# Values of the dilated attention from seven products, with turns, waits, banks and first loads moved, in a four-stage network on one Trainium2 core

## The chip, the cores and the metric

The kernel runs on one core of one Trainium2 chip. The time is that of one execution on the device, in microseconds (us), from the first instruction to the last. It is given as the median of several runs. Everything is computed in float32. The engines of a core are named as the profile names them: PE is TensorE (matrix products and transposes), with PEld for its weight loads; DVE is VectorE; ACT is ScalarE; POOL is GpSimd; SP is SyncE, which here only issues DMA transfers. A "bank" is one of the eight banks of PSUM, into which PE writes 128 x 512 values; "arena" is one big SBUF tensor that holds everything else, so that rows of the trace call nearly every operand by that name.

## The reference, cut to what matters

256 tokens of width 1024 go through two layers of a block whose mixer adds an mLSTM branch and a dilated attention, each followed by a SwiGLU, then through a windowed attention with 256 context tokens and a gated linear attention (GLA), each with an MLP of 4096. Every stage is modulated by rows computed from a condition vector `c`.

```python
c_act = jax.nn.silu(c)
h = layer_norm(x)
for l in range(DEPTH):                                  # DEPTH = 2
    ada = (c_act @ w_ada[l] + b_ada[l])[:, None, :]     # 6 x 1024 values
    sh1, sc1, g1, sh2, sc2, g2 = jnp.split(ada, 6, axis=-1)
    u = h * (1.0 + sc1) + sh1
    y = mixer(u, ...)
    h = layer_norm(DN_ALPHA * h + g1 * y, ...)
    u = h * (1.0 + sc2) + sh2
    h = layer_norm(DN_ALPHA * h + g2 * swiglu(u, w1[l], w3[l], w2[l]), ...)

# mixer: z = u @ w_in; y_a = mlstm_branch(...) @ w_a; y_b = dilated_attention(qkv_a) @ w_b
#        (sigmoid(g_a) * y_a + sigmoid(g_b) * y_b) @ w_out
def dilated_attention(qkv, slopes):       # three patterns: strides 1, 4, 16; 8 heads of 64 each
    qkv = qkv.reshape(B, S, 3, N_PATTERNS, ATT_SLOTS, ATT_HEAD_DIM)
    ...                                   # banded softmax of each pattern, then a softmax over patterns
```

The *values* of the dilated attention are `u @ w_in` for 3 x 512 columns, one group of 512 for each pattern: 256 tokens x 1024 times 1024 x 1536.

## The kernel before

**Work by stage.** One program is written out by hand for each engine, without loops on the device. Each engine runs its list in order, and semaphores tie the lists. The names in the waits are those of steps: `VA 0 full` is PE's last matmul of the tile VA 0, `VA 0 drained` the copy of its bank. PE's list sets the order. A layer goes: first values of the mLSTM ("VM", `values_of`) while the first panels of weights arrive by columns k of the contraction; the gate tile "G"; queries and keys with a convolution by DVE ("S 0" is the first score tile behind it); twelve tiles of queries and keys of the dilated attention ("AQK n"), beside which run pieces of the mLSTM (`minis`, called after each n); then the **value stage**, below; gates and outputs; SwiGLU with `up` panels; the down projection.

**Weights.** They come by SP's DMA as half panels of 4 x 512 columns (1 MB) into a ring of 7. PE frees a panel when it has run its last matmul on it.

**Seven products.** The gates, the up panels and most MLPs are computed with Strassen's scheme: the 2 x 2 blocks of the product come from 7 products of sums instead of 8 products. The order of the products is `ORDER = (1, 2, 4, 5, 7, 6, 3)`. For each panel there are four sums of weight blocks, 128x1024 each: sums 5 and 7 are made by POOL (`gate_weight_sums`, L3474 and its like), 6 and 3 by DVE (`panel_sums`); and DVE makes four sums of token blocks once (`token_sums`) and adds up the results from the banks (`first_sum`, 1 operation, and `product_sums`, 6). Products 6 and 3 overwrite weight blocks that products 1 and 2 have read.

**Value stage before.** `va(j, w)` computes one of six tiles: 128 tokens x 512 columns with 8 matmuls over 512 columns, straight from the weights, and ACT copies each bank. Between them stand the scores (`scores(u)`, u is a pair of slots, tt one of two token halves), the transposed probabilities (`turned(u)`) and the products with the values (`values(u)`). DVE runs a loop over four pairs of slots: maxima, probabilities (`probs n`), and, from the third pair on, a gate panel.

**Turns.** A turn is a piece of `c_act @ w_ada`, done by DVE: two operations of 128x1028 from a slot of weights (four where two condition vectors are needed). POOL issues the load of each slot when DVE has freed it (`ada_free`). POOL's weight sums stand in the same list, at the load numbers given in GATE_JOBS and FIRST_UP_JOB. Where DVE's turns stand is given by MINI_TURNS (after AQK tile n), by `beside_mix(1)` at the end of each pair of slots, by tuples in WA and WB, and by UP_TURNS (after up panel `at`, layer 1 only).

**Start.** `silu(c)` is a Sigmoid by ACT and a product by DVE. The first eight turns are made panel by panel (`ft` 0 to 7), each followed by a modulated column of tokens. After ft 1 DVE raises `first_free`; with that POOL issues the other condition vectors and the first two loads for turns.

**Seams.** Where a stage begins, its tokens are normalised, transposed into a bank by PE, and scaled and shifted out of it column by column, four columns by ACT and four by DVE. `drained(...)` waits for all four.

The lines of the trace: L601 is every matmul, L599 every transpose, L2268 DVE's tensor_tensor (sums), L2271 its tensor_scalar, L2274 its scalar_tensor_tensor (turns among them), L1543 and L1546 ACT's functions and plain bank copies, L3474/L3476 POOL's sums for the up panels, L3490/L3492 those for the gates, L3538 POOL's loads for turns. In the trace a matmul in float32 is two instructions.

```python
ADA_EARLY = (4, 8)                       # turns ahead of the gate tile, by layer
UP_TURNS = (3, 6)
MINI_TURNS = (2, 4, 6, 8, 9, 11)
```

## Time and profile before

| | before |
|---|---|
| median of 3 runs | 2246.53 us (2246.24 to 2246.94) |
| profiled execution, time | 2250.32 us |
| profiled execution, span | 2248.5 us |
| PE busy | 2213.8 us, 98% |
| DVE busy | 1427.2 us, 63% |
| ACT busy | 502.4 us, 22% |
| POOL busy | 287.0 us, 13% |
| clock granted to TensorE, mean | 0.998 |

The profile follows one execution. Its span leaves out what lies before the first and behind the last instruction. "Busy" of PE is an upper bound of useful work: the ends of matmuls are modelled. In a timeline a row is a stretch of like instructions of an engine: its start, its length, line, operation, form and count; the square brackets give the engine's idle time just before it, and what ended it. PEclk is the clock granted to TensorE as a part of full speed.

### The profile page before, as it was taken

The numbers are of one execution on the slowest core, as the hardware profiler recorded it, in microseconds if no ns is written. First come the engines' busy times: TensorE is split into PE (matmuls) and PEld (weight loads), VectorE is DVE, ScalarE is ACT, GpSimd is POOL, SyncE is SP. The second block draws the span as 40 slices with busy tenths as digits, with TensorE's granted clock in tenths as the row PEclk, the third lists the DMA queues.
The fourth block names the chain that finished last, engine by engine and source line by source line (L and its number), as shares of the span: only waits on it lengthen the run. The fifth ranks groups of instructions, "written<-read, shape, count | busy, mean of one in ns | idle before, by whom it ended". The sixth has DMA issues, their size and how long they took to land. (4 is left out here: it accounts for less than half of the span.)

```text
span 2248.5 us, 29974 instructions
## 1 busy us (share of the span) xinstructions
PE 2213.8 (98%) x11968; PEld 1805.9 (80%) x11968; DVE 1427.2 (63%) x2593; ACT 502.4 (22%) x1104; POOL 287.0 (13%) x181
## 2 busy tenths in 40 slices
PE   7999999999999999999999999999999999999998
PEld 5788599799868885888998655588888887778987
DVE  5685453645656566756656877775575777556655
ACT  1213230100012222201110376321200023343300
POOL 0000121331000001223220000000000002002442
PEclk9999999999999999999999999999999999999999
DMA  9995546444576655465655511433443533235542
GB/s 392 324 301 190 189 162 220 169 163 157 196 282 200 237 188 206 160 232 185 193 194 170 188 38 38 160 113 131 139 143 132 210 139 131 75 131 188 187 161 84
DMA packets 179769, 398.91 MB, mean 177 GB/s; under 512 B 21168, under 2 KB 25648, under 8 KB 176560
## 3 DMA queue, kind: packets, MB, share of 16 engines
q1 hardware_dynamic: 136736, 285.03, 36.3%
q0 software_dynamic: 24080, 93.69, 12.2%
q10 hardware_dynamic: 18816, 18.27, 2.5%
q8 instruction: 96, 1.57, 0.3%
q14 instruction: 41, 0.34, 0.0%
HBM read 395.87 MB, written 1.11 MB: 177 GB/s over the span
## 5 line engine op out<-in xcount | busy, mean ns | idle before, releaser
L601 PE MATMUL bank<-arena 128*128 128x256 f32 (+4 forms) x11384 | 2154.2, 358 | 13.2 <-ACT arena L1543 6.0
L601 PEld LDWEIGHTS bank<-arena 128*128 128x128 f32 (+2 forms) x11384 | 1739.9, 188 | 404.3 <-issue 211.8
L2268 DVE TENSOR_TENSOR arena<-arena 128x1024 f32<-128x1024 f32 (+8 forms) x576 | 479.2, 848 | 186.2 <-PE bank L601 148.3
L1543 ACT ACTIVATE arena<-arena 128x512 f32<-128x512 f32 (+5 forms) x443 | 222.6, 525 | 791.9 <-DVE arena L2268 405.2
L2274 DVE SCALAR_TENSOR_TENSOR arena<-arena 128x1028 f32<-128x1028 f32 (+6 forms) x367 | 315.5, 876 | 89.8 <-DMA arena<-in_w_ada 63.7
L2268 DVE TENSOR_TENSOR arena<-arena,bank 128x256 f32<-128x256 f32 (+2 forms) x383 | 172.5, 476 | 184.6 <-PE bank L601 173.6
L3538 POOL DMA_DIRECT2D arena<-in_w_ada x88 | 62.8, 714 | 1484.4 <-DVEq L2283 1441.5
L1543 ACT ACTIVATE arena<-bank 128x256 f32<-128x256 f32 (+3 forms) x165 | 67.3, 423 | 553.8 <-PE bank L601 552.1
L1546 ACT ACTIVATE arena<-bank 128x512 f32<-128x512 f32 (+1 forms) x165 | 89.2, 597 | 307.0 <-PE bank L601 270.7
L2268 DVE TENSOR_TENSOR arena<-bank,arena 128x512 f32<-128x512 f32 (+1 forms) x86 | 56.3, 666 | 157.8 <-PE bank L601 143.1
L2274 DVE SCALAR_TENSOR_TENSOR arena<-bank,arena 128x254 f32<-128x254 f32 (+2 forms) x184 | 78.1, 469 | 54.5 <-ACT arena L1543 27.4
L2271 DVE TENSOR_SCALAR arena<-arena 128x512 f32<-128x512 f32 (+6 forms) x258 | 81.2, 344 | 24.8 <-ACT arena L1543 18.2
L599 PEld LDWEIGHTS bank<-arena 128*128 128x128 f32 x584 | 68.0, 143 | 28.1 <-issue 24.2
L599 PE MATMUL bank<-arena 128*128 128x128 f32 x584 | 74.3, 275 | 11.6 <-DVE arena L2271 11.4
L2274 DVE SCALAR_TENSOR_TENSOR junk<-arena 128x1028 bf16<-128x1028 f32 x64 | 79.7, 1245 | 6.0 <-DMA arena<-in_w_ada 1.7
L1543 ACT ACTIVATE arena<-bank,arena 128x128 f32<-128x128 f32 (+2 forms) x138 | 57.4, 484 | 84.2 <-PE bank L599 37.5
L3474 POOL TENSOR_TENSOR arena<-arena 128x1024 f32<-128x1024 f32 x20 | 48.4, 2420 | 180.8 <-DMA arena<-in_w 86.2
L2271 DVE TENSOR_SCALAR arena<-bank,arena 128x256 f32<-128x256 f32 (+1 forms) x112 | 46.3, 468 | 26.8 <-PE bank L599 14.0
L1543 ACT ACT_TABLE_LOAD x47 | 60.3, 1283 | 2.6 <-PEq L3609 1.2
L2274 DVE SCALAR_TENSOR_TENSOR arena<-arena,bank 128x512 f32<-128x512 f32 (+1 forms) x40 | 24.5, 644 | 43.4 <-PE bank L601 42.6
L3476 POOL TENSOR_TENSOR arena<-arena 128x1024 f32<-128x1024 f32 x20 | 51.2, 2562 | 1.6
L3505 POOL TENSOR_TENSOR arena<-arena 128x1024 f32<-128x1024 f32 x14 | 35.4, 2526 | 87.0 <-PE bank L601 73.1
(39 smaller groups left out, 257.2 us busy)
## 6 DMA issues: line engine op xcount, KB each, us to landing
arena<-in_w_ada POOLq DMA_DIRECT2D x88, 1028.0 KB, 5.8
arena<-in_w_in SPq DMA_DIRECT2D x84, 1024.0 KB, 8.1
arena<-in_w SPq DMA_DIRECT2D x56, 1024.0 KB, 6.8
arena<-in_w_mlp_in SPq DMA_DIRECT2D x32, 1024.0 KB, 7.2
arena<-in_w_mlp_out SPq DMA_DIRECT2D x32, 1024.0 KB, 7.3
arena<-in_w_gla SPq DMA_DIRECT2D x12, 1024.0 KB, 7.0
arena<-in_w_ada SPq DMA_DIRECT2D x16, 514.0 KB, 19.4
arena<-in_w_a SPq DMA_DIRECT2D x8, 1024.0 KB, 7.1
```

What stands on the lines that cost most here:

```text
L599: ins = nc.tensor.transpose(out, lhsT, rhs)
L601: ins = nc.tensor.matmul(out, lhsT, rhs, start=start, stop=stop)
L1543: return nc.scalar.activation(out, x, f, **kw)
L1546: return nc.scalar.activation(out, tile(key)[:, :out.free_size()], f)
L2268: return V.tensor_tensor(out, x, y, op)
L2271: return V.tensor_scalar(out, x, s1, s2, op0, op1) if op1 is not None else V.tensor_scalar(out, x, s1, None, op0)
L2274: return V.scalar_tensor_tensor(out=out, in0=x, scalar=s, in1=y, op0=op0, op1=op1, **kw)
L3474: nc.gpsimd.tensor_tensor(up_sum(at), a21, a22, ALU.add).then_inc(up_sums_made, 1)
L3476: nc.gpsimd.tensor_tensor(a21, a11, a21, ALU.subtract).then_inc(up_sums_made, 1)
L3505: nc.gpsimd.tensor_tensor(wsum, a21, a22, ALU.add).then_inc(mlp_sums_made, 1)
L3538: pool.dma_start(adaw[:, n % ADA_SLOTS], half_source(job, q)).then_inc(ada_in[n % ADA_SLOTS], 16)
```

## The change

1. **Values.** `va` gives way to `value_products(g, order)`: the 512 columns of each pattern g are made with seven products of 4 matmuls over 256 columns. Tokens are split in halves for g = 0 and by even and odd place for g = 1 and 2. POOL makes two weight sums for each g (`value_panel_sums`), DVE two (`value_weight_sums`), four more token sums ("classes"), and seven additions from banks; ACT copies one bank for each g. The scores, transposes and value products are placed anew among them. POOL's sums for the first gates now wait for `probs 3` and `probs 5`.
2. **Turns.** More of them stand beside the AQK tiles (layer 0: nine instead of six, layer 1: seven, three of them in halves, instead of six), fewer in the loop over slots (one, at the last pair, instead of four). In layer 1 the two whole turns beside the up panels become ten halves. `token_sums("gates")` goes ahead of the last piece of mLSTM.
3. **Start.** Silu by ACT alone; `first_free` after ft 3; the banks of VM in layer 0 are those of T shifted by one.
4. **Gate tile of layer 0.** Three turns ahead of it and the fourth behind "gates abs".
5. **Seams.** Layer 1: the first three columns are waited for one by one. Seam to the GLA ("next"): the first tile of gates is computed by token half and column, the first half ahead of the second transposes; DVE's share of the first half is moved ahead of the last addition of the MLP.
6. **Windowed attention.** At t = 1 ACT drains query 3 and the turned probabilities before `latent_exps(1, 1)`.
7. **GLA.** `decays(3)` goes from the start of h = 2 to behind its state.

```diff
-UP_TURNS = (3, 6)
-MINI_TURNS = (2, 4, 6, 8, 9, 11)
+UP_TURNS = {at: (at % 2,) for at in range(10)}
+MINI_TURNS = ({n: (0, 1) for n in (0, 1, 2, 3, 4, 5, 6, 8, 9)},
+              {**{n: (0, 1) for n in range(4)}, **{n: (n % 2,) for n in range(4, 10)}})
+VALUE_JOBS = {23: [(0, g) for g in range(NPAT)], 45: [(1, g) for g in range(NPAT)]}
...
+        class_x = [UT[:, KH * j:KH * j + KH, r::RES] for j in range(2) for r in range(RES)]
...
-                        if k == 0:
+                        if k < 3:
+                            pe.wait_ge(act_done, AC.at(f"T 0 column {k}"))
+                        else:
                             drained("T 0 0")
...
+                def value_products(g, order, over=None):
+                    q = quarters(value_panel_at(l, g))
+                    x, sums, tag = value_tokens(g)
+                    ops = {1: (q[0], x[0]), 2: (q[1], x[2]), 4: (q[3], sums[4]), 5: (gate_sum, sums[5]),
+                           7: (q[2], sums[7]), 6: (q[0], sums[6]), 3: (q[1], x[3])}
+                    for i in order:
...
+                        if i in (6, 3):
+                            pe.wait_ge(dve_done, DV.at(f"VA {g} w{i}"))
+                        if i in (5, 7):
+                            pe.wait_ge(value_sums_made, values_made(l, g, i))
+                        for k in range(KH):
+                            mm(ps[:, :2 * P], ops[i][1][:, k, :], ops[i][0][:, k, :], start=(k == 0), stop=(k == KH - 1),
+                               done=key if k == KH - 1 else None)
...
                     if u == 0:
-                        for j in range(6):
-                            pe.wait_ge(act_done, AC.at(f"VA {j} drained"))
+                        for g in range(NPAT):
+                            pe.wait_ge(dve_done, DV.at(f"VA {g} c12"))
...
                 w = panel()
-                va(0, w)
+                value_products(0, ORDER[:2])
                 scores(0)
-                va(1, w)
+                value_products(0, ORDER[2:])
                 release(w)
                 w = panel()
-                va(2, w)
+                value_products(1, ORDER[:4])
                 turned(0)
+                value_products(1, (6, 7, 3), "PT 1 1")
+                release(w)
                 scores(1)
-                va(3, w)
+                w = panel()
+                value_products(2, (1, 2, 4, 5, 6, 7, 3))
                 release(w)
-                w = panel()
-                va(4, w)
-                va(5, w)
-                release(w)
+                scores(2, (0,))
+                values(0)
                 turned(1)
-                values(0)
-                scores(2)
+                scores(2, (1,))
...
-                    func(csig[0], crow[:, 0, :D], ACT.Sigmoid).then_inc(act_done, AC.step("sigmoid 0"))
+                    func(crow[:, 0, :D], crow[:, 0, :D], ACT.Silu).then_inc(act_done, AC.step("cond 0"))
...
-                        if ft == 1:
+                        if ft == 3:
                             dve.wait_ge(dve_done, DV.count)
                             dve.sem_inc(first_free, 1)
...
+                beside_gates = 3 if l == 0 else ADA_EARLY[l]
+                early_turns(turns[:beside_gates])
                 dve.wait_ge(pe_done, PE.at("G full"))
...
+                early_turns(turns[beside_gates:ADA_EARLY[l]])
                 dve.wait_ge(act_done, AC.at("softplus"))
...
+                token_sums("classes", class_x, [class_tokens[i] for i in (5, 6, 4)], False, class_tokens[7])
+                value_weight_sums(0)
+                first_sum("VA 0", value_blocks(0), value_read(0))
                 for u in range(SLOTS // 2):
...
+                    if u == 0:
+                        for _ in product_sums("VA 0", value_blocks(0), value_read(0)):
+                            pass
+                    if u == 1:
+                        value_weight_sums(2)
+                        first_sum("VA 2", value_blocks(2), value_read(2))
...
-                    beside_mix(1)
+                    if u == 3:
+                        turn_part((0, 1))
...
+            gate_columns(0, range(4))
+            normed_transposes("next", range(1, 2), None)
...
-                if h in (1, 2):
-                    decays(h + 1)
+                if h == 1:
+                    decays(2)
...
+                if h == 2:
+                    decays(3)
...
+                if p == 0:
+                    pool.wait_ge(dve_of[f"layer {l}"], DV.of(f"layer {l}", f"probs {3 + 2 * b}"))
...
-                    pool.wait_ge(pe_of[f"layer {l}"], PE.of(f"layer {l}", "S 3 full"))
+                    pool.wait_ge(pe_of[f"layer {l}"], PE.of(f"layer {l}", f"VA {NPAT - 1} 5 full"))
```

**PE, the value stage of a layer**, in program order; L599 (L621 after) are transposes (`turned`), L601 (L623) matmuls, a count is of matmuls as written in the program. The rows with 64 partitions or 128 columns are scores and value products. Before:

```order
L601 MATMUL bank<-arena 128x512 x8
L601 MATMUL bank<-arena 128x256 x2
L601 MATMUL bank<-arena 128x128 x4
...
L601 MATMUL bank<-arena 128x512 x16
L599 MATMUL bank<-arena 128x128 x16
...
L601 MATMUL bank<-arena 128x512 x24
L599 MATMUL bank<-arena 128x128 x16
```

After, the same stretch:

```order
L623 MATMUL bank<-arena 128x256 x10
L623 MATMUL bank<-arena 128x128 x4
...
L623 MATMUL bank<-arena 128x256 x36
L621 MATMUL bank<-arena 128x128 x16
L623 MATMUL bank<-arena 128x256 x14
...
L623 MATMUL bank<-arena 128x256 x30
L623 MATMUL bank<-arena 128x128 x4
```

The 48 matmuls over 512 columns are gone, and 84 over 256 stand in their place (counted in the rows with the scores' own, which have that width too); the scores of the first pair now stand behind 8 short matmuls, and the second transposes behind the first products with values.

**DVE, the value stage of layer 0**, from the token sums for the gates on. L2268 (L2320) are sums, L2274 (L2326) with 128x1028 a turn, with 512 the sum of a score bank and its bias; L2864 (L2936) a maximum, 128x512 of L2271 (L2323) probabilities. Before:

```order
L2274 SCALAR_TENSOR_TENSOR arena<-arena 128x1028 x2
L2268 TENSOR_TENSOR arena<-arena 128x512 x4
L2274 SCALAR_TENSOR_TENSOR arena<-arena,bank 128x512 x2
L2864 TENSOR_REDUCE arena<-arena 128x2
...
L2870 RECIPROCAL arena<-arena 128x2
L2271 TENSOR_SCALAR arena<-arena 128x512 x2
L2274 SCALAR_TENSOR_TENSOR arena<-arena 128x1028 x2
```

After:

```order
L2320 TENSOR_TENSOR arena<-arena 128x512 x4
L2326 SCALAR_TENSOR_TENSOR arena<-bank,arena 128x256 x2
L2320 TENSOR_TENSOR arena<-arena 128x512 x4
L2320 TENSOR_TENSOR arena<-arena 128x4x256 x2
L2320 TENSOR_TENSOR arena<-arena,bank 128x256
L2326 SCALAR_TENSOR_TENSOR arena<-arena,bank 128x512 x2
...
L2320 TENSOR_TENSOR arena<-arena,bank 128x256 x6
L2948 RECIPROCAL arena<-arena 128x2
...
L2323 TENSOR_SCALAR arena<-arena 128x512 x2
L2320 TENSOR_TENSOR arena<-arena 128x4x256 x2
L2320 TENSOR_TENSOR arena<-arena,bank 128x256 x7
```

The turns have left, and token sums, two weight sums and seven additions for each pattern have come, the first two patterns' around the first pair of slots.

**PE, the seam to the GLA.** L599 (L621) with 128x128 are the transposes of the normalised tokens, eight for each token half; the matmuls are the first tile of gates, behind them the second (16 more). Before:

```order
L599 MATMUL bank<-arena 128x128 x16
L601 MATMUL bank<-arena 128x256 x32
```

After:

```order
L621 MATMUL bank<-arena 128x128 x8
L623 MATMUL bank<-arena 128x128 x8
L621 MATMUL bank<-arena 128x128 x8
L623 MATMUL bank<-arena 128x128 x24
L623 MATMUL bank<-arena 128x256 x16
```

The first tile is now 32 matmuls over 128 columns instead of 16 over 256, and 8 of them stand between the two sets of transposes.

## Rows read from the trace of the kernel before

**Rows 1.** The page: span, and PE's busy time, share, instructions.

```profile
span 2248.5 us, 29974 instructions
PE 2213.8 (98%) x11968; PEld 1805.9 (80%) x11968; DVE 1427.2 (63%) x2593; ACT 502.4 (22%) x1104; POOL 287.0 (13%) x181
```

**Rows 2.** Timeline of PE, two unbroken stretches: start, length, operation, count.

```profile
1018.73 7.46 PE L601 MATMUL bank<-arena 128*128 128x512 f32 x17
1026.03 0.60 PE L599 MATMUL bank<-arena 128*128 128x128 f32 x4
...
1977.79 6.64 PE L601 MATMUL bank<-arena 128*128 128x256 f32 x30
```

**Rows 3.** Windows, the value stage of layer 0: PE, PEld, DVE, ACT, POOL busy.

```profile
229.50:300.00 70.50, 70.50 (x372) 44.97 (x371) 35.86 (x65) 19.64 (x44) 11.75 (x7) 1.00 0.45 165
```

**Rows 4.** Timeline of DVE, same stage.

```profile
233.14 0.88 DVE L2274 SCALAR_TENSOR_TENSOR arena<-bank,arena 128x256 f32<-128x256 f32 x2 [4.23 <-PE bank L599]
...
236.46 2.75 DVE L2268 TENSOR_TENSOR arena<-arena 128x512 f32<-128x512 f32 x4
...
246.85 0.88 DVE L2271 TENSOR_SCALAR arena<-arena 128x512 f32<-128x512 f32 x2
...
293.63 2.55 DVE L2268 TENSOR_TENSOR arena<-arena 128x1024 f32<-128x1024 f32 x2
296.09 0.41 DVE L2268 TENSOR_TENSOR arena<-arena,bank 128x256 f32<-128x256 f32 x1
```

**Rows 5.** Timeline of POOL, same stage: a weight sum.

```profile
295.03 3.36 POOL L3490 TENSOR_TENSOR arena<-arena 128x1024 f32<-128x1024 f32 x1 [24.56 <-DVE arena L2268]
```

**Rows 6.** Timeline at 430, an up panel: DVE's and POOL's sums side by side.

```profile
430.15 2.36 POOL L3474 TENSOR_TENSOR arena<-arena 128x1024 f32<-128x1024 f32 x1 [8.28 <-DVE arena L2268]
430.30 6.59 DVE L2268 TENSOR_TENSOR arena<-arena 128x1024 f32<-128x1024 f32 x2
```

**Rows 7.** The start: timeline of PE, and a window (after the clock: DMA share, GB/s).

```profile
20.59 1.98 PE L601 MATMUL bank<-arena 128*128 128x512 f32 x4 [1.21 <-ACT arena L1543]
...
45.00:80.00 35.00, 35.00 (x143) 24.03 (x144) 17.69 (x40) 8.33 (x12) 2.10 (x3) 1.00 1.03 400
```

**Rows 8.** Timeline, gate tile and convolution of layer 0: DVE, then PE.

```profile
79.41 1.23 DVE L2274 SCALAR_TENSOR_TENSOR arena<-arena 128x1028 f32<-128x1028 f32 x1 [1.60 <-DMA arena<-in_w_ada]
...
84.26 0.19 DVE L2274 SCALAR_TENSOR_TENSOR arena<-arena 128x32 f32<-128x32 f32 x1 [1.84 <-ACT arena L1543]
...
146.18 2.00 PE L601 MATMUL bank<-arena 128*128 128x256 f32 x8 [1.80 <-ACT arena L1543]
```

**Rows 9.** Timeline, seam to layer 1.

```profile
626.68 1.50 ACT L1543 ACTIVATE arena<-bank,arena 128x128 f32<-128x128 f32 x4 [2.48 <-DVE arena L2268]
...
628.28 1.52 PE L601 MATMUL bank<-arena 128*128 128x512 f32 x3 [1.26 <-issue]
```

**Rows 10.** Timeline, value stage and an up panel of layer 1: PE waits for DVE.

```profile
926.19 1.02 PE L601 MATMUL bank<-arena 128*128 128x128 f32 x7 [0.57 <-DVE arena L2268]
...
1087.16 4.51 DVE L2268 TENSOR_TENSOR arena<-arena 128x1024 f32<-128x1024 f32 x2 [0.21 <-DVE arena L2274]
...
1091.82 0.35 PE L601 MATMUL bank<-arena 128*128 128x128 f32 x1 [1.27 <-DVE arena L2268]
```

**Rows 11.** Timeline of PE, windowed attention.

```profile
1308.47 1.09 PE L601 MATMUL bank<-arena 64*128 64x512 f32 x3 [1.01 <-DVE arena L2271]
```

**Rows 12.** Seam to the GLA: timeline of PE, and a window (clock third from the end).

```profile
1843.92 1.09 PE L599 MATMUL bank<-arena 128*128 128x128 f32 x8 [0.44 <-DVE arena L2271]
...
1846.27 14.01 PE L601 MATMUL bank<-arena 128*128 128x256 f32 x56 [1.25 <-ACT arena L1543]
...
1848.00:1850.00 2.00, 2.00 (x6) 1.55 (x6) 1.76 (x8) 0.31 (x2) 0.00 (x0) 0.50 0.98 363
```

**Rows 13.** Timeline, GLA head 2.

```profile
1977.51 2.34 DVE L3271 TENSOR_TENSOR_SCAN arena<-arena 128x512 f32<-128x512 f32 x2
...
1985.67 2.61 PE L601 MATMUL bank<-arena 128*128 128x256 f32 x11 [1.24 <-DVE arena L2274]
```

More of the change, by code:

```diff
@@ L3134, in fast_mlp @@
                     diagonals(1)
+                if after:
+                    modulated2(after, 0, 0)
                 next(sums, None)
                 if after:
[L3137 removed]
+                    for tt in range(1, t):
                         modulated2(after, tt, 0)
```

203 lines of the change are left out of this document (126 added, 77 removed).

## Prediction, before the changed kernel was run

> **What bounds the kernel now.** I read the page first: PE is busy for 2213.8 of 2248.5 us [rows 1], so only two things can pay: fewer columns through PE, and the 35 us in which it stands. Then I read the forms of PE in long stretches [rows 2] for what a column costs, and last the timeline around each stop of PE, asking which wait ended last. A stop of idle time g costs g + 0.16 us, since the last matmul before it is drawn with a tail: a stretch of 17 is drawn 7.46 us long while the next begins 7.30 us after its start [rows 2]. Below, stops are given with that tail. DVE has slack on average, but in the value stage it works 35.9 of 70.5 us, and POOL 11.8 [rows 3]: there the change puts its new sums.
>
> **Values.** [Rows 2] give 7.30 / 17 = 0.429 us for an instruction of 512 columns and (6.64 - 0.16) / 30 = 0.216 for one of 256. Before, a layer has 6 x 8 x 2 = 96 of the first, 41.2 us; after, 3 x 7 x 4 x 2 = 168 of the second, 36.3 us. That is 4.9 a layer, **-9.9** in all, if PE never waits for the sums. These are, for each layer, by rows of the same forms [rows 4]: four class sums of 128x512 at 0.69 (2.8), six weight sums of 128x1024 at 1.23 (7.4), 21 additions from banks at 0.42 (8.8): 19.0 us of DVE; three turns leave the slot loop (2.3 each in layer 0: 6.9; four operations, 5.1 each, in layer 1). DVE comes to 35.9 + 19.0 - 6.9 = 48 of about 65 us. POOL gets 6 sums of 2.36 to 3.36 [rows 5, 6], 14 to 20 us more. ACT loses six bank copies and gains three short ones: nothing.
>
> I laid the new lists side by side, with PE's first value matmul at 0. DVE: gate sums to 1, class sums to 6 (with POOL in the way), w6 and w3 of pattern 0 at 7.5 and 8.7 (PE wants w6 at about 10.6), first slots to 14.5, additions to 17.0, probabilities at 19.1 (PE wants them at 21.0), w6 of pattern 1 at 20.3 (22.8), its additions to 28.5, where PE wants a bank at 28.0; w6 of pattern 2 at 35.9 (37.0), probabilities 39.9, last additions 42.7, wanted at 43.1. PE ends the stage at 47.8. So it fits, with margins of 0.4 to 1.1 us at three places, and one is short by 0.2 to 0.5. I set +0.8 a layer, **+1.6**, for these.
>
> The known disturbance is two engines in the arena at once: two DVE sums take 6.59 instead of 2.5 us beside POOL's sums, and a POOL sum that meets DVE's takes 3.36 instead of 2.36 [rows 4 to 6]. So a sum that meets POOL costs up to 2.1 more. The class sums meet it (counted), and DVE then waits for POOL's pair anyway before w6. The probabilities (tensor_scalar, two operations in 0.88 [rows 4]) come behind POOL's pair in my schedule, and the new wait of POOL's gate sums on `probs 3` and `probs 5` keeps those off them; queued behind that wait are the loads of turns, of which the loop now needs one.
>
> No row shows a tensor_scalar beside POOL. The Trainium skill, "SBUF — State Buffer", section "Who interferes with whom", says that tensor_scalar in its two-port mode also takes the shared ports and then blocks, or is blocked, for a whole instruction. By the rows that would be up to one POOL sum, 2.36 to 3.36, on `probs 1` in each layer against a margin of 1.9: it is a rival below. The same page's rule that a sum from a bank does not contend would make the additions safe; this trace shows none above 0.42 to 0.44.
>
> **More turns beside the AQK tiles.** Three more in layer 0 (2.3 us each), in layer 1 one more. Behind the last of them DVE idles for 4.23 us, waiting for PE [rows 4], and a turn delays it by 2.3, or by 2.6 for a half with two vectors: I take no cost, bounds 0 to 1 us. If the cover goes, PE stops by the difference.
>
> **Start.** The product by DVE, 1.23 us, leaves the chain to the first turns, but these wait for weights; I take 0.2 to 0.3 of it. The stop ahead of the first 512-column matmuls, 1.21 + 0.16 [rows 7], goes, since the bank it takes was drained earlier. But the memory system is full here (share 1.03, 400 GB/s at 45 to 80 us [rows 7]), and what PE gains may be waited for at a later column; moving the first loads behind ft 3 gives their bytes to the panels at first and takes them back later. **Gate tile**: the turn in the way of "gates abs" waited 1.60 for its load and took 2.3; abs comes some 2.3 to 4 us earlier, the softplus of ACT hides behind the fourth turn instead of stalling DVE for 1.84, and the whole convolution on DVE moves up. PE's stop at its end is 1.80 + 0.16 [rows 8]. This stop absorbs what the start gains: both parts together can give between 0.4 (DVE waits at the loads of its other turns instead) and 3.3 (both stops, nothing else late). I take **-1.5**, near the stop's own size, since the loads are what DVE waits for there.
>
> **Seam to layer 1.** ACT starts its four columns at 626.68 and needs 1.50 for them, and PE waits for all, 1.26 + 0.16 [rows 9]. With a wait for each column it starts one column in, about 0.45 after 626.68, and each further column (0.35) is ready before four matmuls of 0.43 are through: **-1.0** (0.8 to 1.2).
>
> **Two stops behind turns in layer 1.** PE waits 0.57 + 0.16 for a weight sum that stood behind a turn of 5.1 us, and 1.27 + 0.16 behind one beside an up panel, where the sum met POOL as well (two sums in 4.51 us) [rows 10]. The first turn is gone, the second is cut into halves of 2.6, one per panel: **-2.1** (-2.1 to -0.8, if a half still meets POOL's sum).
>
> **Windowed attention.** PE waits 1.01 + 0.16 [rows 11] for a bank whose query ACT drains behind exponentials; drained ahead of them, it is in time: **-1.1**. Bounds -1.2 to 0, since the exponentials, and what PE builds on them, come later by the drains.
>
> **Seam to the GLA.** PE stops 0.44 + 0.16 ahead of the second transposes and 1.25 + 0.16 ahead of the gates; then its granted clock falls from 1.00 to 0.50, the lower level of 1.2 GHz, in which a 256-column matmul instruction takes some 0.42 instead of 0.216 for 3.4 us [rows 12]. That costs 1.9 more. After, eight matmuls of 0.225 (1.8 us) fill the wait between the transposes, and the first tile costs 64 x 0.112 = 7.2 instead of 32 x 0.216 = 6.9. PE has no stop over 1 us then. I let the fall of the clock go too: -0.5 -1.4 -1.9 +0.2, **-3.6**; if the clock still falls, -1.8.
>
> **GLA.** DVE's two scans of `decays(3)` take 2.34 us, and with the operations around them more, ahead of the state that PE waits for, 1.24 + 0.16 [rows 13]. Moved behind it, they free more than the stop: **-1.4**. Head 3's gates come later for it; where they took half of the gain back it would be -0.7.
>
> **Sum.** -9.9 + 1.6 - 1.5 - 1.0 - 2.1 - 1.1 - 3.6 - 1.4 = -19.0. The profiled execution took 2250.3, so 2231.3 on its scale; the median of the runs, 2246.5, is 3.8 lower: **2227.5**, I say 2228.
>
> **Rivals.**
> (a) *The value stage waits on DVE.* If POOL blocks the probabilities (2.4 to 3.4 us against a margin of 1.9) or the class sums run longer, everything behind in DVE's list is late, and the last additions have 0.4 to spare: 1 to 3.3 us a layer more. For it: margins smaller than one POOL sum; against: POOL has six sums in 48 us and is kept off the later probabilities. 2230 to 2235. Chance 0.22.
> (b) *The clock falls at the seam all the same*, since the engine still had short matmuls and transposes ahead of it: +1.8, 2229.5. Chance 0.2; it joins with the forecast or (a).
> (c) *Memory takes back the start*: +1.1, 2229. It stays in the range.
> (d) *Only the values arrive.* The moved waits turn up at the next thing that is late: -9.9 + 1.6 and half of the rest, about 2233 to 2238. Chance 0.15.
> (e) *Slower.* DVE's list in the value stage becomes the bound: if every one of the ten sums with two arena operands met POOL (2.1 each, 21 us a layer) DVE would have 69 of 65 us to do, and the last additions, on which `values(0)` and all behind it wait, would come some 10 us or more late in each layer. From 9.5 us a layer the change loses; at 12, 2251. Against it: one overlap costs one of the two engines, and POOL itself works 14 to 20 us of the stage. Chance 0.04.
> (f) *The change does not do what it says*: PE's count of 512-column matmuls must fall by 192 instructions; the order of the program shows it, so this is 0.01.
>
> **How the numbers follow.** Forecast as summed, 2225 to 2231: 0.57 (with (b) or (c) inside). (a) 0.22, (d) 0.15, (e) and (f) 0.05. A rest of 0.01 lies below 2225. The range 2224 to 2237 leaves out (e) and the ends of (d) and of the forecast. 0.2% is 4.5 us, about what a measurement of this kernel tells from no change: faster from 2242.0 down. Of (d) 0.02 and of (e) 0.02 end within 0.2%: faster 0.92, same 0.04, slower 0.04.
>
> **What would show it.** Right: in the two value stages no PE stop over 0.5 us, and PE's first gate product 4 to 5 us earlier after its first value matmul; no stop over 0.5 us at the seam to layer 1, behind the first convolution, in the up panels and at head 2 of the GLA; at the seam to the GLA clock 1.00 throughout. Wrong: PE waiting on `VA 1 w6`, on VA 1's banks or on `VA 2 c12` (then (a) or (e)); DVE sums of 3.2 us among the class or weight sums of patterns 1 and 2; a probability operation longer than 0.5 us; new idle before the ft columns at 25 to 45 us (then (c)).

## The result, and the profile after

| | before | after |
|---|---|---|
| median | 2246.74 us (2246.24 to 2247.05, 4 runs) | 2230.13 us (2228.39 to 2230.42, 4 runs) |
| ratio | | 0.9925, 95% interval 0.9907 to 0.9942 |
| profiled execution, time | 2250.32 us | 2228.39 us |

The change saves 16.6 us; 2228 was forecast, within 2224 to 2237. The two profiled executions differ by 21.9 us, though, 5 more than the medians: the one of before is longer than any run that its median is taken from, the one of after is the shortest of its four. Where those 5 lie is the main thing that the experiments found.

The page after; the second line answers to [rows 1]:

```profile
span 2226.6 us, 30478 instructions
PE 2201.4 (99%) x12144; PEld 1833.1 (82%) x12144; DVE 1472.0 (66%) x2652; ACT 500.7 (22%) x1100; POOL 315.3 (14%) x193
```

PE stood for 35 us, now for 25; its busy time fell by 12.4, DVE's rose by 45. Timelines of PE after, around the places of [rows 7, 9, 10, 11, 13] and of the stop behind the convolution in [rows 8] (the second row, from a second profile of the changed kernel):

```profile
15.65 6.70 PE L623 MATMUL bank<-arena 128*128 128x256 f32 x23 [1.41 <-ACT arena L1594]
...
133.69 14.67 PE L623 MATMUL bank<-arena 128*128 128x256 f32 x67
...
619.19 3.24 PE L623 MATMUL bank<-arena 128*128 128x512 f32 x7 [0.22 <-issue]
...
905.75 9.74 PE L623 MATMUL bank<-arena 128*128 128x128 f32 x91
...
1070.81 9.43 PE L623 MATMUL bank<-arena 128*128 128x128 f32 x83
...
1291.10 3.06 PE L623 MATMUL bank<-arena 64*128 64x512 f32 x16
...
1959.74 8.58 PE L623 MATMUL bank<-arena 128*128 128x256 f32 x39
```

The stretches run through where PE had stood; only 0.22 us is left at the seam to layer 1, and the first stop, 1.41, which the change does not touch. The value stages of layers 0 and 1, in the columns of [rows 3], from the first value matmul to the first gate product:

```profile
229.30:276.30 47.00, 46.93 (x283) 40.94 (x282) 35.92 (x62) 11.98 (x29) 18.04 (x8) 1.00 0.45 152
833.60:880.60 47.00, 46.93 (x283) 40.94 (x282) 35.90 (x62) 11.98 (x29) 18.06 (x8) 1.00 0.44 151
```

PE works 46.93 of 47.00 us in both. DVE has 35.9 us of work in these 47, where it had as much in 70.5 us [rows 3]. DVE's timeline in layer 0:

```profile
230.36 7.25 DVE L2320 TENSOR_TENSOR arena<-arena 128x512 f32<-128x512 f32 x6
...
264.25 2.56 DVE L2320 TENSOR_TENSOR arena<-arena 128x1024 f32<-128x1024 f32 x2
266.72 0.41 DVE L2320 TENSOR_TENSOR arena<-arena,bank 128x256 f32<-128x256 f32 x1
267.05 0.16 DVE L2948 RECIPROCAL arena<-arena 128x2 f32<-128x2 f32 x1
267.24 0.88 DVE L2323 TENSOR_SCALAR arena<-arena 128x512 f32<-128x512 f32 x2
...
270.21 2.08 DVE L2320 TENSOR_TENSOR arena<-arena,bank 128x256 f32<-128x256 f32 x5 [0.57 <-PE bank L623]
```

The first row has the four class sums and the two weight sums of pattern 0: 2.75 + 2.46 = 5.2 us by [rows 4], 7.25 here, since POOL's pair runs beside it. The last additions end at 272.3; PE needs them at 272.8. That is a margin of half a microsecond; the schedule had given 0.4.

The seam to the GLA, PE and then the window that answers to [rows 12]:

```profile
1826.21 2.02 PE L623 MATMUL bank<-arena 128*128 128x128 f32 x16 [0.26 <-ACT arena L1594]
1828.07 1.04 PE L621 MATMUL bank<-arena 128*128 128x128 f32 x8
1828.94 3.29 PE L623 MATMUL bank<-arena 128*128 128x128 f32 x28
...
1828.00:1830.00 2.00, 2.00 (x21) 2.00 (x20) 1.54 (x5) 1.29 (x4) 0.00 (x0) 1.00 1.05 407
```

One stop of 0.26 us is left, and the granted clock stays at 1.00.

### The profile page after: what moved, and what is told of

Its sections match the earlier page's. It is cut to its first block and busy times, and to the rows that moved or that the text cites. A ratio compares the mean times of both kernels' runs of the same rounds, so it can differ in the third digit from the quotient of the medians.

```text
span 2226.6 us, 30478 instructions
## 1 busy us (share of the span) xinstructions
PE 2201.4 (99%) x12144; PEld 1833.1 (82%) x12144; DVE 1472.0 (66%) x2652; ACT 500.7 (22%) x1100; POOL 315.3 (14%) x193
## 3 DMA queue, kind: packets, MB, share of 16 engines
q1 hardware_dynamic: 136736, 285.03, 36.3%
q0 software_dynamic: 24080, 93.69, 12.4%
## 5 line engine op out<-in xcount | busy, mean ns | idle before, releaser
L623 PE MATMUL bank<-arena 128*128 128x256 f32 (+6 forms) x11560 | 2141.8, 354 | 4.3 <-ACT arena L1594 1.7
L623 PEld LDWEIGHTS bank<-arena 128*128 128x128 f32 (+2 forms) x11560 | 1767.3, 188 | 357.5 <-issue 164.4
L2320 DVE TENSOR_TENSOR arena<-arena 128x1024 f32<-128x1024 f32 (+8 forms) x593 | 499.5, 857 | 185.6 <-PE bank L623 147.2
L2326 DVE SCALAR_TENSOR_TENSOR arena<-arena 128x1028 f32<-128x1028 f32 (+7 forms) x367 | 320.7, 891 | 89.7 <-DMA arena<-in_w_ada 64.6
L2320 DVE TENSOR_TENSOR arena<-arena,bank 128x256 f32<-128x256 f32 (+2 forms) x425 | 189.1, 470 | 188.6 <-PE bank L623 174.9
L2320 DVE TENSOR_TENSOR arena<-bank,arena 128x512 f32<-128x512 f32 (+1 forms) x86 | 56.3, 666 | 148.4 <-PE bank L623 134.9
L1597 ACT ACTIVATE arena<-bank 128x512 f32<-128x512 f32 (+1 forms) x153 | 82.2, 596 | 252.4 <-PE bank L623 203.2
L2326 DVE SCALAR_TENSOR_TENSOR arena<-bank,arena 128x254 f32<-128x254 f32 (+2 forms) x184 | 78.0, 469 | 36.9 <-ACT arena L1594 22.0
L2323 DVE TENSOR_SCALAR arena<-arena 128x512 f32<-128x512 f32 (+6 forms) x258 | 84.3, 356 | 24.8 <-ACT arena L1594 18.3
L621 PEld LDWEIGHTS bank<-arena 128*128 128x128 f32 x584 | 67.9, 143 | 26.0 <-issue 22.6
L621 PE MATMUL bank<-arena 128*128 128x128 f32 x584 | 74.5, 276 | 11.2 <-DVE arena L2323 11.0
L2326 DVE SCALAR_TENSOR_TENSOR junk<-arena 128x1028 bf16<-128x1028 f32 x64 | 80.0, 1251 | 5.7 <-DMA arena<-in_w_ada 1.5
L2323 DVE TENSOR_SCALAR arena<-bank,arena 128x256 f32<-128x256 f32 (+1 forms) x112 | 46.4, 469 | 20.6 <-PE bank L623 9.1
L2326 DVE SCALAR_TENSOR_TENSOR arena<-arena,bank 128x512 f32<-128x512 f32 (+1 forms) x40 | 24.6, 643 | 17.0 <-PE bank L623 9.0
```

Of the source, the lines that this page charges most:

```text
L621: ins = nc.tensor.transpose(out, lhsT, rhs)
L623: ins = nc.tensor.matmul(out, lhsT, rhs, start=start, stop=stop)
L1597: return nc.scalar.activation(out, tile(key)[:, :out.free_size()], f)
L2320: return V.tensor_tensor(out, x, y, op)
L2323: return V.tensor_scalar(out, x, s1, s2, op0, op1) if op1 is not None else V.tensor_scalar(out, x, s1, None, op0)
L2326: return V.scalar_tensor_tensor(out=out, in0=x, scalar=s, in1=y, op0=op0, op1=op1, **kw)
```

## The experiments

Every kernel was compared with the kernel before on its own chip. Four groups ran, each on one chip: the first four kernels, the next four, the next three, and the last.

**1. Both kernels again, unchanged** (c_before, c_after).

> The kernel before, unchanged, for a second profile. In the first its execution took 2250.3 us, 3.8 over the median of its other runs, and its clock fell to 0.50 for 3.4 us at the seam to the gated linear attention (worth about 1.9 us). Theory A: that fall, and some of the stops at the start, happen in some executions only; then this profile shows clock 1.00 at that seam and a span 2 to 4 us shorter. Theory B: the fall is in every execution and the 3.8 us is of the profiled execution as such; then the profile again shows 0.50 there. Time in either case 2246.5 within 0.5, ratio 1.000.

> The changed kernel, unchanged, beside the kernel before on one chip. Its profiled execution took 2228.4 us, the other three 2229.9 to 2230.4. Theory A (the stops differ between executions): the profile has a stop of 1 to 2 us of the matrix engine that the first one lacks, most likely in the first 150 us, where weights arrive just in time. Theory B (same stops in each): same timeline within 0.3 us. Time 2230 within 0.5, 16.5 us under the kernel before.

Measured: before 2246.32 us (ratio to itself 0.9998, 0.9990 to 1.0007), after 2228.96 (ratio 0.9920, 0.9906 to 0.9933). The second profile of the kernel before is 4.0 us shorter in span than the first. Its seam to the GLA, PE and a window:

```profile
1843.91 8.44 PE L601 MATMUL bank<-arena 128*128 128x256 f32 x38 [1.25 <-ACT arena L1543]
...
1846.00:1848.00 2.00, 2.00 (x11) 1.75 (x10) 1.76 (x7) 0.00 (x0) 0.00 (x0) 1.00 0.73 267
```

The same stop of 1.25, but clock 1.00 and 11 matmuls in 2 us instead of 6 [rows 12]. And at the end of the convolution, where the first profile has 1.80 us of idle [rows 8], PE runs through:

```profile
129.71 20.64 PE L601 MATMUL bank<-arena 128*128 128x256 f32 x93
```

Theory A for the kernel before: the fall of the clock and the stop behind the convolution belong to some executions. The two profiles of the changed kernel agree within 0.3 us everywhere, as in theory B; but both are of its shortest executions (2228.39 and 2228.13 us), so they say nothing of those that take 2229.6 to 2230.4.

To find what each place contributes, I matched PE's instructions of two profiles one to one and took the difference of their start times; it changes in steps, and each step belongs to a place:

| place | forecast | first pair of profiles | second pair |
|---|---|---|---|
| start and gate tile | -1.5 | -3.7 | -1.6 |
| values, layer 0 and layer 1 | -8.3 | -9.3 | -9.2 |
| seam to layer 1 | -1.0 | -0.7 | -0.8 |
| two stops behind turns | -2.1 | -2.4 | -2.4 |
| windowed attention | -1.1 | -1.3 | -1.3 |
| seam to the GLA | -3.6 | -3.3 | -1.6 |
| GLA, head 2 | -1.4 | -1.4 | -1.4 |
| sum | -19.0 | -22.0 | -18.3 |

Against this sum some 0.3 us comes back at the first additions of the GLA's MLP, where PE waits 0.88 us for a sum of POOL and waited 0.52 before. The values, most of the start and gate tile, and the seam to the GLA were also undone one at a time, below; the two stops behind turns, the windowed attention, the seam to layer 1 and the GLA's head 2 were not undone one by one, and their shares rest on these profiles.

**2. Two edits of the start, and the one of the gate tile, undone** (u_start, u_gates).

```diff
 u_start
-    tiles[v_keys[n]] = open_tile(v_keys[n], None if l else marks.get(... f"T {(n + 1) % 4}"), 0))
+    tiles[v_keys[n]] = open_tile(v_keys[n])
...
-    if ft == 3:
+    if ft == 1:
 u_gates
-    beside_gates = 3 if l == 0 else ADA_EARLY[l]
+    beside_gates = ADA_EARLY[l]
```

> The changed kernel with two start edits undone: first_free after ft 1 again, so that the condition vectors and the first two loads of turns are issued some 10 us earlier, and the banks of VM in layer 0 not shifted. My theory: a stop of 1.4 us comes back at 19 to 20.6 us, and since the stop behind the convolution (2.0 us before) no longer absorbs it, up to 1.4 of it stays: 2230.5 to 2231.6. Rival 1 (memory sets the pace until 150 us): the stop is made up for by later waits for columns, 2230.1. Rival 2: the earlier loads also delay a column of weights, and 2 us or more are lost: over 2232.

> The changed kernel with all four early turns ahead of the gate tile again in layer 0. My theory: gates abs comes 2.3 to 4 us later, DVE stands 1.84 us for the softplus again, and the convolution's end falls behind; the stop of the matrix engine at about 142 us returns in full, since the start no longer slows that engine: 2232.0 to 2232.6 (1.9 to 2.5 more). Rival: the loads of turns set the convolution's pace (DVE stood up to 3.0 us for them behind the first pieces), so the earlier start is eaten by them: within 0.5 of the changed kernel.

Measured: u_start 2230.04 us (ratio 0.9931, 0.9919 to 0.9944) and u_gates 2230.08 (0.9926, 0.9912 to 0.9940), each 1.1 over the changed kernel beside it (0.9920, 0.9906 to 0.9933). The intervals overlap, so by the medians alone neither 1.1 is clear of noise. The profile of u_gates, DVE at the softplus and PE behind the convolution:

```profile
83.16 0.19 DVE L2326 SCALAR_TENSOR_TENSOR arena<-arena 128x32 f32<-128x32 f32 x1 [1.84 <-ACT arena L1594]
...
144.02 4.17 PE L623 MATMUL bank<-arena 128*128 128x256 f32 x18 [1.52 <-ACT arena L1594]
```

The softplus stall and the stop are back, 1.7 us with its tail, and the profiled execution (2230.08) lies 1.95 over that of c_after (2228.13); both have full clock from 14 us on. So the mechanism and its size, 1.9 to 2.5, are as argued in this pair, but the forecast of the time, 2232.0 to 2232.6, was missed by 1.9. In u_start's profile the expected stop at 19 us is not there. Its first 256-column matmuls took 0.43 us each instead of 0.216 for longer (full clock came at 20.2 us instead of 14.1), which cost 2.1 us, and its first transposes started 0.5 us later; nothing was left to wait for. How much of the 1.1 is the edit's was not separated; rival 2 (over 2232) is out, and between the first theory and rival 1 it is inconclusive.

**3. The values alone undone** (u_values): `va`, its places among scores and transposes, and no value sums, as before; all else as after.

> The changed kernel with only the values of the dilated attention made as before (six tiles of 512 columns, the old places of scores and transposes, no value sums); the moved turns, seams and start stay. My theory: the seven products are worth 4.6 us in each layer, as the two profiles show between the first value matmul and the first gate product, and the other edits stand by themselves: 9.2 more than the changed kernel, about 2238.3 where that takes 2229. Rival 1: part of that gain belongs to the turns that left the slot loop (they took 2.3 to 5.1 us of DVE each), then less than 8 is lost. Rival 2: the new sums slow something outside the stage (turns and loads in a row behind it), then the whole costs less than the stage shows: under 2237.

Measured: 2238.67 us; its profiled execution took 2236.8, 8.7 over that of c_after, 2228.1. PE in layer 0, the first value matmul and the third transposes, first in u_values, then in the changed kernel:

```profile
228.69 22.92 PE L623 MATMUL bank<-arena 128*128 128x512 f32 x72
...
296.62 1.91 PE L621 MATMUL bank<-arena 128*128 128x128 f32 x16
```

```profile
229.18 21.32 PE L623 MATMUL bank<-arena 128*128 128x256 f32 x112
...
292.49 1.91 PE L621 MATMUL bank<-arena 128*128 128x128 f32 x16
```

That is 67.93 us against 63.31, in the kernel before 67.93 too. So the stage is 4.6 us longer, and by the same two rows in layer 1 (905.23 - 837.30 against 896.82 - 833.51) 4.6 there. The ratio to the kernel before is 0.9963 (0.9950 to 0.9975). So the seven products are worth about 9, and the rest of the change about 8. Both rivals fall by the median.

**4. The seam to the GLA undone** (u_next): all transposes first, the first gate tile in 256 columns, DVE's share behind the last additions.

> The changed kernel with the seam to the gated linear attention as before (all transposes, then the first gate tile in 256 columns by groups of four columns; DVE's part behind the last additions). Theory A (what two profiles of the kernel before say): the stops of 0.35 to 0.6 and 1.4 us come back, the clock falls in some executions only: 1.4 to 1.8 more, 2230.5 to 2230.8, and the profile may or may not show 0.50 at about 1828 us. Theory B (the prediction's): stops and clock go together, 3.6 more: 2232.6, and 0.50 is in the profile.

Measured: 2229.49 us; the profile, PE at the seam:

```profile
1827.47 1.09 PE L621 MATMUL bank<-arena 128*128 128x128 f32 x8 [0.44 <-DVE arena L2306]
1829.82 2.40 PE L623 MATMUL bank<-arena 128*128 128x256 f32 x10 [1.25 <-ACT arena L1577]
```

Both stops of [rows 12] are there, to the hundredth, and no fall of the clock; aligned with c_after the seam costs 1.3 us. Of the mechanism theory A holds. Its time, 2230.5 to 2230.8, does not: the median is only 0.5 over c_after's, on another chip and within both intervals. (The profiled execution took 2230.86; it has full clock only from 19.0 us on, which cost it another 1.9.) The prediction's 3.6 needed an execution in which the clock falls.

**5. POOL's waits on the probabilities taken out** (x_pool).

```diff
-                if p == 0:
-                    pool.wait_ge(dve_of[f"layer {l}"], DV.of(f"layer {l}", f"probs {3 + 2 * b}"))
```

> The changed kernel without POOL's new waits on probs 3 and probs 5, so that its sums for the first gates start as soon as products 5 of the last values are done, beside DVE's probabilities (tensor_scalar, 0.49 us each alone). Theory A (contention of tensor_scalar with a POOL sum): a probability takes up to 2.4 us more, and with 0.5 us to spare behind it PE stops 1.9 us or more before the first values(0) in each layer: 2232 to 2235. Theory B (only operations with two arena operands meet POOL): probabilities stay at 0.49 and time at 2229 within 0.7.

Measured: 2238.36 us, 9.4 over the changed kernel on another chip and 8.1 under the kernel before on its own. The profile, DVE, POOL and PE in layer 0, and a window:

```profile
268.49 4.77 DVE L2323 TENSOR_SCALAR arena<-arena 128x512 f32<-128x512 f32 x2
...
268.13 2.35 POOL L3584 TENSOR_TENSOR arena<-arena 128x1024 f32<-128x1024 f32 x1 [11.35 <-DVE arena L2320]
270.56 2.41 POOL L3586 TENSOR_TENSOR arena<-arena 128x1024 f32<-128x1024 f32 x1
...
277.08 2.81 PE L623 MATMUL bank<-arena 128*64 128x256 f32 x24 [2.92 <-DVE arena L2320]
...
278.00:280.00 2.00, 2.00 (x19) 1.67 (x16) 0.00 (x0) 0.08 (x1) 0.00 (x0) 0.51 1.05 394
```

Two probability operations that take 0.88 us alone take 4.77, each until the sum of POOL that runs beside it is over; PE then stands 2.92 us for the last additions, and its clock falls to half 0.9 us behind the stop (0.51 in this window). Aligned, the stop costs 3.0 and the clock 1.6 us in layer 0, 3.2 and 1.4 in layer 1. The mechanism of theory A holds; its time, 2232 to 2235, was too low, because the whole of both sums was waited for and the stop took the clock with it. The Trainium skill, "SBUF — State Buffer", section "Who interferes with whom", says that tensor_scalar can take the shared ports and that the later instruction blocks fully; this trace agrees, 4.77 us against 0.88.

**6. Layer 0's turns back in their old places** (u_turns).

```diff
-MINI_TURNS = ({n: (0, 1) for n in (0, 1, 2, 3, 4, 5, 6, 8, 9)},
+MINI_TURNS = ({n: (0, 1) for n in (2, 4, 6, 8, 9, 11)},
...
-                    if u == 3:
+                    if u == 3 or l == 0:
```

and POOL's jobs in layer 0 three loads earlier.

> The changed kernel with layer 0's turns back in their old places (six beside the AQK tiles, four in the slot loop), beside the new sums. My theory: DVE has 0.5 to 2 us to spare at the last additions and the weight sums of patterns 1 and 2, a turn takes 2.3; the one ahead of the stage and the one behind the first pair are not hidden: PE stops 1.5 to 3 us in all, 2230.5 to 2232. Rival: the idle times that DVE has in the stage (2.9, 1.4, 0.8, 3.6 us) take them all: 2229 within 0.5, and then moving the turns was no condition of the gain.

Measured: 2236.15 us, some 7 over the changed kernel on another chip. DVE, POOL, then PE, in the profile:

```profile
231.53 1.22 DVE L2326 SCALAR_TENSOR_TENSOR arena<-arena 128x1028 f32<-128x1028 f32 x1
...
234.12 9.80 DVE L2320 TENSOR_TENSOR arena<-arena 128x512 f32<-128x512 f32 x6 [0.21 <-DVE arena L2326]
...
246.74 1.85 DVE L2323 TENSOR_SCALAR arena<-arena 128x2 f32<-128x2 f32 x1
...
235.07 2.36 POOL L3602 TENSOR_TENSOR arena<-arena 128x1024 f32<-128x1024 f32 x1
...
240.33 1.97 PE L623 MATMUL bank<-arena 128*128 128x256 f32 x8 [0.56 <-POOL arena L3604]
244.31 3.72 PE L623 MATMUL bank<-arena 128*128 128x256 f32 x16 [2.01 <-DVE arena L2320]
249.33 7.16 PE L623 MATMUL bank<-arena 128*128 128x256 f32 x32 [1.29 <-DVE arena L2326]
...
273.07 8.40 PE L623 MATMUL bank<-arena 128*128 128x256 f32 x60 [0.44 <-DVE arena L2320]
...
284.70 5.47 PE L623 MATMUL bank<-arena 64*128 64x256 f32 x49 [1.34 <-DVE arena L2326]
```

The turn ahead of the stage (2.3 us) delays the class sums, and they now meet both of POOL's sums in full: 9.80 instead of 7.25. POOL itself is late, too: its pair starts 4.5 us behind the first value matmul (230.53) where it had started 1.1 us ahead of it (228.11, 229.18), since a load that waits for the turn's slot stands before it in POOL's list. PE stands at product 7, at product 6 and at the next bank. That third stop ends a chain in which a tensor_scalar of 128x2, 0.17 us alone, took 1.85 beside a sum of POOL. PE stands again at the last additions and behind the second transposes, there after a turn's operation that took 3.39 us instead of 1.22 beside POOL. By aligned starts these stops cost 6.6 us in one layer. My theory named part of the mechanism and sized it at 1.5 to 3: it added the turns, but not the contention and the late loads that they bring. In this kernel, moving layer 0's turns is a condition of the values' gain there.

**7. Idle products ahead of the first transposes; POOL's sums earlier** (c_after_b, v_warm, v_pool).

```diff
 v_warm
+                if l == 0:
+                    pe.wait_ge(x_in[0], 16)
+                    warm(8, H[:, 0, :P], "warm")     # matmuls of 128 columns, nobody reads their bank
+                    pe.wait_ge(cst_in, 16)
+                    warm(6, ident)
...
                     transposes("T")
+                    warm(6, ident)
...
+                dve.wait_ge(pe_done, PE.at("warm"))
 v_pool
+                if (job, q) == (DEPTH + 1, ADA_LAST[-1]):
+                    mlp_sums(0, 1)
                 pool.wait_ge(ada_free, n + 1)
```

> The changed kernel again, as the measure for the two beside it. In eight profiles full clock was granted to the matrix engine either at 13.6 to 14.4 us or at 18.6 to 20.2 us, and the times of the changed kernel fall in two groups 1.4 us apart (2228.1 to 2228.4, and 2229.6 to 2230.4). Theory: these are the same two cases. Then this profile shows one of the two pairs: early and about 2228.2, or late and about 2229.7.

> The changed kernel with 14 idle products of the matrix engine ahead of the first transposes (8 as soon as the first tokens have landed, at about 5 us, 6 with the identity, which lands at about 9) and 6 behind them; nothing reads their bank. Theory: a late grant of full clock costs 1.4 us because nothing waits behind the first 256-column products any more; with work ahead of them the grant is early in every execution: one group of times at about 2228.2, median 0.7 to 1.4 under the changed kernel beside it where that is mostly late. Rival: what sets the grant is not the engine's work in the first 10 us; two groups stay, or it stays late: no change, or 0.5 more from the added products.

> The changed kernel with POOL's first pair of sums for the GLA's MLP ahead of its last load for a turn (that load waits for a turn of DVE, and the sums behind it). In the profiles PE stops there for 1.04 and 0.58 us, waiting for these two sums, which start at 2046.3 though DVE was through with their area at 2041.5. Theory: both stops go, 1.6 less. Rival: the sums now meet DVE's turn (two arena operands), which then takes up to 2.4 more, the load comes 1 to 2 us later, and PE waits for DVE's additions or the next panel's sums instead: no change, or 1 more.

Measured: c_after_b 2228.47 us (2228.16 to 2234.66, 5 runs), v_warm 2227.48 (2227.10 to 2227.51, 4 runs; ratio to the kernel before 0.9911, 0.9896 to 0.9925), v_pool 2231.30 (0.9934).

c_after_b was granted full clock at 15.1 us and took 2228.29: the early case and the short time, as in the theory. How the two cases look in a window of PE from 16 to 18 us, c_after first, then u_next:

```profile
16.00:18.00 2.00, 2.00 (x11) 1.74 (x10) 1.66 (x3) 0.00 (x0) 0.00 (x0) 1.00 0.99 414
```

```profile
16.00:18.00 2.00, 2.00 (x6) 1.63 (x5) 1.87 (x3) 0.00 (x0) 0.00 (x0) 1.00 0.95 395
```

Eleven matmul instructions against six in the same 2 us. Aligned, the late grant (18.6 to 20.2 us) cost 1.7 to 2.1 us in the four profiles that have it (u_start, u_next, x_pool, u_turns). (The clock column says 1.00 in both: it has no record ahead of the first change, and the spacing tells.) In v_warm PE works from 4.79 us on, and full clock was there at 8.6. Two rows of its start, and its first stop in the GLA's MLP; behind them, for that stop, c_after:

```profile
4.79 3.78 PE L743 MATMUL bank<-arena 128*128 128x128 f32 x16 [4.79 <-DMA arena<-in_x]
...
15.52 4.98 PE L623 MATMUL bank<-arena 128*128 128x256 f32 x19 [1.82 <-ACT arena L1605]
...
2048.16 2.02 PE L623 MATMUL bank<-arena 128*128 128x128 f32 x16 [0.52 <-POOL arena L3629]
```

```profile
2048.80 2.02 PE L623 MATMUL bank<-arena 128*128 128x128 f32 x16 [0.88 <-POOL arena L3617]
```

Its four times lie within 0.4 us and below every run of the changed kernel beside it, 1.0 under that one's median; the two intervals overlap. But the clock does not explain this 1.0. The median of c_after_b is itself of the early case, and the theory had put v_warm at 2228.2. The first 256-column matmul starts at 15.52 us, as in c_after (15.56), since it waits for ACT in both. Aligned with c_after_b, v_warm gains 0.2 us at the start and 0.4 at the stop in the GLA's MLP, which its edit does not touch and which is 0.86 to 0.88 in every other profile of the changed kernel's family but v_pool's; why, is open. What speaks for the theory is that no late time is among the four; that the grant is early in all of them is inferred, one was profiled. It has the lowest median of the case.

v_pool, DVE, POOL and PE at the GLA's MLP, and a window:

```profile
2041.78 3.35 POOL L3617 TENSOR_TENSOR arena<-arena 128x1024 f32<-128x1024 f32 x1 [5.95 <-DVE arena L2320]
...
2042.85 3.38 DVE L2326 SCALAR_TENSOR_TENSOR arena<-arena 128x1028 f32<-128x1028 f32 x1
2045.22 3.23 POOL L3619 TENSOR_TENSOR arena<-arena 128x1024 f32<-128x1024 f32 x1
...
2053.56 12.69 PE L623 MATMUL bank<-arena 128*128 128x128 f32 x97 [2.02 <-DVE arena L2320]
...
2050.00:2060.00 10.00, 7.98 (x57) 7.82 (x57) 9.72 (x11) 3.01 (x8) 6.96 (x3) 0.83 0.64 246
```

v_pool's median is 2.8 over c_after_b's. The two stops on POOL went, and the rival came, larger than expected: both halves of DVE's turn take 3.4 us instead of 1.2 beside POOL, DVE's additions come 4.3 us later, PE stands 2.02 us for them, and the clock falls again (0.83 on average here).

**8. The idle products in the kernel before** (b_warm).

> The kernel before with the same 14 + 6 idle products around its first transposes. It has a stop of 0.9 to 1.4 us at 19 us, which the changed kernel lacks. Theory: that stop takes up a late grant of full clock, so that an early grant in every execution gives the kernel before nothing or at most 0.5 us (2245.9 to 2246.6), where it gave the changed kernel 1.0; then part of what the start edits brought is visible only with an early grant. Rival: a late grant costs the kernel before 1.4 us as well, in about half of its executions: then its median falls by 0.7 or more, to 2245.8 or less, with its runs within 0.4 of each other.

Measured: 2246.07 us (2245.41 to 2248.27, 11 runs; ratio 0.9999, 0.9990 to 1.0008). The kernel before took 2246.59 beside it; the difference of 0.5 is at the edge of the theory and not clear of noise, and the spread of the runs is no narrower. Full clock came at 9.8 us, and the stop ahead of the 512-column matmuls is still there:

```profile
15.93 3.69 PE L601 MATMUL bank<-arena 128*128 128x256 f32 x16 [1.74 <-ACT arena L1554]
20.39 1.99 PE L601 MATMUL bank<-arena 128*128 128x512 f32 x4 [0.78 <-ACT arena L1554]
```

The rival (0.7 or more, runs within 0.4) is not borne out. Aligned with c_before, nothing is gained by the time of the convolution's end (0.04 us). This fits the theory that the stop covers for a late clock, but does not show it: all three profiles of the kernel before have the early grant (9.8 to 14.2 us). The nearest case is u_start, with the old banks and a late grant, where this stop is absent.

## Why the prediction was right, and where it was off

**Right, in mechanism and size.** The gain a layer from column counts: from start to start, the 96 instructions of 512 columns take 41.5 us in the kernel before and the 168 of 256 columns 36.9 in the one after, 4.6 for 4.9 (the forecast had 36.3 for the latter). Also the two stops behind turns (-2.4 for -2.1), the attention (-1.3 for -1.1), the GLA (-1.4). Rival (a) with its two halves: x_pool shows the contention, u_turns the thin margins. The kernel avoids both by placement, as the schedule had it.

**The values' allowance, too large.** The +1.6 for tight places in the value stages was mis-sized: PE stood 0.07 us in 47, and the two stages gave -9.2 to -9.3 for -8.3. Most of what is missing to -9.9 lies in the steps between 256-column instructions, 0.220 us on average where 0.216 had been read, and not in stops. The schedule held to half a microsecond; the +0.8 a layer was distrust without a row.

**The step that failed: carrying the sum from the profiled execution to the median.** I took the stops of one profile, 3.8 us over the median of the other runs, and subtracted the same 3.8 from the result. But those 3.8 us were no constant: they were in part the terms that I counted as gains. In the second profile of the kernel before, which is 4.0 shorter, the clock does not fall at the seam (1.7 less to gain there), the stop behind the convolution is missing (1.8 less), and the start is 0.6 shorter. The fall had also been priced too high: 1.9, where 3.4 us at half the clock can cost 1.7. On its own scale the sum of 19.0 was too small (22.0 by the first pair of profiles); against an ordinary execution it is right within a microsecond (18.3), for partly wrong reasons: the seam gave 1.6 instead of 3.6, the values 0.9 more, the two stops behind turns and the attention 0.5 more. In times: 2231.3 stood for the profiled execution, which took 2228.39, and 2227.5 for the median, which came at 2230.13; each is off by under 3 us, in opposite directions. That 2228 came so near the median is in part luck.

**Start and gate tile** were forecast at -1.5, with 3.3 as the outer bound. -1.6 and -3.7 came, in two pairs of profiles. The size seems to depend on how long the loads take in the execution that one looks at (not tested); the bound was the sum of the two stops, and in the first pair some 0.4 us of short waits between the columns went as well.

**The rest, to the median.** The medians moved by 16.6, 17.7 and 18.4 us in three groups, where aligned profiles say 18.3. The difference fits a late grant of full clock at the start (1.4 us between the two groups of times, 1.7 to 2.1 in aligned profiles), if the changed kernel suffers it in some executions and the kernel before hides most of it in its stop (experiments 7 and 8). That is argued, and neither half was profiled. In every one of its three profiles the changed kernel had the early grant; the late case is seen only in u_next, u_start, x_pool and u_turns.

**Seam to layer 1** gave 0.7 to 0.8 for 1.0: 0.22 us of idle is left ahead of the first column, and what else is missing lies in waits between the columns too short to be told apart here.

## What to carry to other kernels

Before stops of one profile are priced, ask how far that execution lies from the median, and take a second profile: a stop that is in one of them only is worth its share of executions. When an engine gets extra work in a stage where it has half a microsecond to spare, what is placed beside it matters more than its sum: the same work cost 7 to 9 us more when turns went back into the stage or a POOL sum met the wrong operation. A stop of the matrix engine can bring a slow clock behind it (x_pool, v_pool), and may hide one (not shown here). And where a kernel comes out faster than its theory allows, it pays to align the profiles there too: nearly half of what the idle products gained over the early case came at a stop that they do not touch.

## What the runs showed of the hardware

- A tensor_scalar of 128x512 from SBUF to SBUF waited for the POOL sum of SBUF operands beside it in full: two took 4.77 us instead of 0.88, beside two sums of 2.35 and 2.41 (x_pool, the same in both layers). One of 128x2 took 1.85 instead of 0.17 (u_turns).
- The clock fell to half behind stops of 2.9 us (x_pool, in both layers) and 2.0 us (v_pool), and once behind stops of 0.44 and 1.25 us with eight transpose instructions between them [rows 12]; the same two stops left it at full in three other executions (c_before, u_next, b_warm). Each fall cost 1.4 to 1.7 us.
- Full clock after the start came between 13.6 and 15.1 us or between 18.6 and 20.2, with like work of the engine from 10.5 to 11.3 us on. With idle products it came at 8.6 us in v_warm, where the engine worked from 4.8 on, and at 9.8 in b_warm, from 5.2 on. The Trainium skill, "TensorE: Matmul & The Clock Gate", section "What's actually happening", says that the throttled state is the default, that activity releases it, and that the moment varies by 500 ns. These profiles agree that it varies, but by more: some 5 us lie between the two groups.
